# A product-key expert layer: who makes the low parts of the expert tables, and in what order

## The chip, the cores and the metric

The kernel runs on one core of a Trainium2 chip. Its time is the device time of one execution, in microseconds (us). TensorE multiplies matrices, VectorE, ScalarE and GpSimd work on elements, and SyncE starts most transfers. The engines run side by side and wait for each other by counters (semaphores).

## The reference, cut to what matters

Two layers of a network for 384 tokens (128 of context, 256 latent). Each layer ends with this channel mixer, and the change touches it alone:

```python
def peer_ffn(h, w_query, sub_keys, u_tab, v_tab):
    q = (h @ w_query).reshape(B, L, PEER_HEADS, 2, PEER_QDIM // 2)
    s = jnp.einsum('blhtd,htnd->blhtn', q, sub_keys)
    s1, i1 = lax.top_k(s[..., 0, :], PEER_TOPK)
    s2, i2 = lax.top_k(s[..., 1, :], PEER_TOPK)
    cand = s1[..., :, None] + s2[..., None, :]
    top, pos = lax.top_k(cand, PEER_TOPK)      # of the 16 x 16 sums
    idx = jnp.take_along_axis(cidx, pos, -1)   # expert = i1 * 128 + i2
    g = jax.nn.softmax(top, axis=-1)
    act = jax.nn.gelu(einsum('td,tkd->tk', h, u_tab[idx]))
    return einsum('tk,tkd->td', g * act, v_tab[idx])
```

There are 8 heads, 128 keys on each side, 16384 experts, 16 chosen for each head and token, and a width of 1024.

## The kernel before

The kernel gathers nothing. It computes the activation of all 16384 experts for all 384 tokens, multiplies by a gate that is zero for experts not chosen, and multiplies by the whole value table. The experts go in 128 blocks of 128.

**Split products.** Float32 precision is kept by splitting each operand into a high part (rounded) and a low part (the rest). ScalarE makes the high part of a table block (`high`), another engine the low part (`x - high`), and TensorE then does 24 matmuls for one block (`product`: 8 slices of the width, three products each, lines 976 to 978). Table buffers (`ur` loaded, `uh` high, `ul` low) and the PSUM result (`bank`) are doubled. Afterwards ScalarE applies the gelu and keeps the result in `A`, a ring of `RING` blocks (`gelu`, line 1070).

**The stages of one layer in `mix_experts`**, as TensorE goes through them:
1. 16 query blocks, each with its key scores (line 989). VectorE finds the top 16 as the scores come.
2. The first `FIRST` = 20 expert blocks (numbered from 0 here). Meanwhile VectorE *decodes* the chosen positions (`at_least`, `chosen`, `sum_ranks`, lines 1253 to 1286, "decoding"): large comparisons and sums in float16. Its last step posts `picked`.
3. Three transposes per token tile (line 1017), after which VectorE makes the operands of the gates.
4. The gates, in 48 chunks of 8 tokens. For each chunk VectorE makes *one-hots* in four instructions (`one_hots`, lines 1312 to 1316), TensorE multiplies them in 16 matmuls (`gates`, lines 998 and 999), and ScalarE copies the result out (line 1088) and stores it to memory after every eighth chunk. One block of the tables stands behind every 4 chunks: 12 groups, blocks 20 to 31.
5. A tail of 4 blocks, 32 to 35.
6. 128 *slots*: each multiplies the gated activations of a block by its values (line 1037, 18 matmuls), and in the first 92 slots one more table block (36 to 127) follows.

**Who makes the low parts.** GpSimd makes those of the query blocks and of blocks 0 to 36, in two halves (line 1173). VectorE makes those of blocks 37 to 127 whole, in the slots (`lo_part`, line 160).

**What sets the order.** Each engine runs its own list strictly as written; there is no scheduler. The waits that matter here: `product` of block n waits for its low part (`ulow`, or `ulow2` where VectorE makes it) and for the gelu of block n-2. One-hots are doubled, so `one_hots` of chunk c waits until TensorE has done chunk c-2 (`gated`). `gates` of chunk c waits for its one-hots (`hot`) and for the copy of chunk c-3. SyncE loads block n when the low part of block n-2 is made. ScalarE makes the high part of block n after product n-2.

Of the kernel before, what the change touches and what calls it, by code (L numbers as in the profile page):

```python
# [32 lines left out]
P = 128  # L33
D = 1024
KC = D // P
T = 384
# [770 lines left out]
FIRST, PER, TAIL = 20, 4, 4  # L807
RING = FIRST + NT * PER + TAIL
CT = 8
CHUNKS = P // CT  # L810
HALF = P // 2
SOON = 32
# [50 lines left out]
def mix_experts(nc, s, cx, d, layer, hi, lo, acc):  # L863
# [48 lines left out]
    with nc.Block() as block:  # L912
        @block.sync
        def _(sp):
# [18 lines left out]
            with sp.Fori(0, RING // 2) as i:  # L933
# [3 lines left out]
            sp.wait_ge(gst0, 16 * (NT + 1))  # L937
            value(0, 0)
            value(1, 1)
            sp.wait_ge(ulow, 2 * (J + RING) + 2)  # L940
            table(RING, 0)
            sp.wait_ge(gst1, 16 * (NT + 1))
            gate(0, 0)
            gate(1, 1)
            sp.wait_ge(ulow, 2 * (J + RING) + 4)
            table(RING + 1, 1)

            def slot(z):
                b = z.first % 2
                if z.has(RING + 2):  # L950
                    sp.wait_ge(ulow2, z.n + 1)
                    table(z.n + (RING + 2), b)
                if z.has(2):
                    sp.wait_ge(vlow, z.n + 3)
                    value(z.n + 2, b)
                    sp.wait_ge(applied, z.n + 1)
                    if z.first + 2 >= SOON:
                        sp.wait_ge(gst2, 16 * (NT + 1))
                    gate(z.n + 2, b)
# [4 lines left out]
        def _(pe):  # L964
# [39 lines left out]
            pe.sem_inc(gated, 2)  # L1004
# [20 lines left out]
            with pe.Fori(0, TAIL // 2) as i:  # L1025
                for b in range(2):
                    early(i * 2 + (J + RING - TAIL + b), b)

            def slot(z):
                b = z.first % 2  # L1030
                pe.wait_ge(vlow, z.n + 3)
                pe.wait_ge(wlow, z.n + 1)
                for t in range(NT):
                    w = slice(t * P, (t + 1) * P)
                    for lhs, rhs in ((wh, vh), (wh, vl), (wl, vh)):
                        for c in range(2):
                            mm = pe.matmul(acc[:, 2 * t + c, :], r32(lhs[:, b, w]), r32(rhs[:, b, c * 512:(c + 1) * 512]),  # L1037
                                           start=False, stop=False, skip_group_check=True)
                mm.then_inc(valued, 1)
                if z.has(RING):  # L1040
                    product(z.n + (J + RING), b, ulow2, z.n + 1, whole=True)
# [4 lines left out]
        def _(act):  # L1046
# [25 lines left out]
            def early(n, b, turn):  # L1072

                gelu(n + (J - 1), 1 - b, bass.ds(n - 1, 1))
                high(n + (J + 1), 1 - b, turn)

            def gates(t, u):
                c = t * CHUNKS + u
                if u == 0:
                    act.wait_ge(gst0, t * 16 + 16)  # L1080
                if u == CHUNKS // 2:
                    act.wait_ge(gst1, t * 16 + 16)
                    act.wait_ge(gst2, t * 16 + 16)
                act.wait_ge(gated, c + 3)
                at = u * CT % HALF
                out = stg[:, 2 * u // CHUNKS, :, at:at + CT].rearrange("p k t -> p t k")
                src = acc[:, 2 * (u % 3):2 * (u % 3) + 2, :].rearrange("p b (t k) -> p (b t) k", k=P)
                nc.scalar.activation(out, src, copy, scale=1.0 / GATE_SCALE).then_inc(evacd, 1)  # L1088
                if u == CHUNKS // 2 - 1:
                    act.wait_ge(evacd, c + 4)  # L1090
                    dst = gates_dram[bass.ds(t * 2, 1)].rearrange("a p k c -> p (a k) c")
                    act.dma_start(dst, stg[:, 0]).then_inc(gst0, 16)
                if u == CHUNKS - 1:
                    act.wait_ge(evacd, c + 4)
                    dst = gates_dram[bass.ds(t * 2 + 1, 1)].rearrange("a p k c -> p (a k) c")
                    act.dma_start(dst[:, 0:SOON], stg[:, 1, 0:SOON]).then_inc(gst1, 16)
                    act.dma_start(dst[:, SOON:NKEYS], stg[:, 1, SOON:NKEYS]).then_inc(gst2, 16)

            act.sem_inc(drained, 2)
            act.sem_inc(evacd, 3)  # L1100
            for g in (gst0, gst1, gst2):
                act.sem_inc(g, 16)
# [8 lines left out]
            high(J + 1, 1, J // 2)  # L1111
            with act.Fori(0, FIRST // 4) as i:
                for b in range(2):
                    early(i * 2 + (1 + b), 1 - b, i + (J // 2 + (2 + b) // 2))
            act.wait_ge(sub, 1)
            nc.scalar.activation(ex[:], ex[:], ACT.Exp).then_inc(expd, 1)
            nc.scalar.activation(warm[:], cx.eps[:], ACT.Gelu_apprx_tanh)
            done = FIRST // 4 * 2
            for n in range(done + 1, FIRST):
                early(n, n % 2, (n + 1 + J) // 2)  # L1120
# [3 lines left out]
            with act.Fori(0, NT) as t:  # L1124
                for a in range(PER):
                    early(t * PER + (FIRST + a), a % 2, t * (PER // 2) + (J + FIRST + a + 1) // 2)
                    for u in range(CHUNKS // PER):
                        gates(t, a * (CHUNKS // PER) + u)
# [14 lines left out]
            for n in range(RING - TAIL, RING):  # L1143
                if n == RING - 2:
                    value_high(start, 0)
                if n < RING - 1:
                    early(n, n % 2, (n + 1 + J) // 2)
            gelu(J + RING - 2, 0, bass.ds(RING - 2, 1))
            high(J + RING, 0, (J + RING) // 2, uhigh2)
# [17 lines left out]
        def _(pool):  # L1167
            pool.sem_inc(ulow, 4)
            with pool.Fori(0, (J + RING) // 2) as i:
# [6 lines left out]
        def _(dve):  # L1176
# [34 lines left out]
            find(J - 1, 1)  # L1211

# [58 lines left out]
            chosen(0)  # L1271
            st.done(v.tensor_tensor(pr[:], ge[:], table(1).unsqueeze(1).to_broadcast([P, T, TOPK]), ALU.mult))
            st.settle()
            sum_ranks(row[:])
            st.done(v.tensor_tensor(bd[:], posd[:], row[:].unsqueeze(2).to_broadcast([P, T, 2]), ALU.subtract))
            st.settle()
            at_least(bd, 2)
            chosen(1)
            dve.wait_ge(expd, 1)
# [7 lines left out]
                            den[:].unsqueeze(2).to_broadcast([P, TH, TOPK]), ALU.mult).then_inc(picked, 1)  # L1287
            dve.wait_ge(turned, 1)
# [14 lines left out]
            def one_hots(t, u):  # L1303
                c = t * CHUNKS + u
                b = u % 2
                toks = bass.ds(t * P + u * CT, CT)

                def each(x):
                    return x[:, toks, :].unsqueeze(2).to_broadcast(twos)

                dve.wait_ge(gated, c + 1)
# [27 lines left out]
            def table_low(z, ahead):  # L1339
                b = (z.first + ahead) % 2  # L1340
                dve.wait_ge(uhigh2, z.n + (ahead + 1))
                lo_part(nc, ul[:, b], ur[:, b], uh[:, b]).then_inc(ulow2, 1)

            dve.sem_inc(vlow, 2)
            start = Slot(0, 0)
            dve.wait_ge(evacd, NT * CHUNKS + 3)
            v.memset(acc[:], 0.0)
            value_low(start, 0)
            apply(start, 0)
            table_low(start, 0)  # L1350
            gated_low(start, 0)

            def slot(z):
# [4 lines left out]
                if z.has(RING + 1):  # L1358
                    table_low(z, 1)
# [776 lines left out]
```

## Time and profile before

| | us |
|---|---|
| median of 3 runs | 3905.05 (3904.53 to 3905.38) |
| the profiled execution | 3904.66 |
| its span, first to last instruction | 3902.9 |
| TensorE busy | 3271.5 (84%) |
| VectorE busy | 1951.1 (50%) |
| ScalarE busy | 1202.7 (31%) |
| GpSimd busy | 524.3 (13%) |
| mean granted clock of TensorE | 0.890 of full speed |

In the rows PE is TensorE, PEld its weight loads, DVE VectorE, ACT ScalarE, POOL GpSimd, SP SyncE. Matmul records overlap (a matmul is listed as 0.33 us where the next begins 0.17 us after it), so the pace is read from start to start. The clock has two levels, 0.5 (1.2 GHz) and 1.0 (2.4 GHz). The expert mixer of the first layer runs from 684 to about 1960 us, that of the second from about 2578.

### The profile page before, as it was taken

To read this page: it belongs to the slowest core of one execution; us is meant where nothing else is said; L and a number is where in the kernel's file an instruction comes from. 1 tells how busy PE (TensorE), PEld (TensorE's weight loads), DVE (VectorE), ACT (ScalarE), POOL (GpSimd) and SP (SyncE) were. 2 spreads that over 40 slices of the span, in tenths; PEclk is the share of its full clock that TensorE was granted. 3 is DMA by queue.
4 is the path that set the end of the run, shared out by engine and by line. 5 is a ranking of instruction groups with operands and counts; after the bars stand their busy time and mean duration, and the time that the engine had idled before them with its cause. 6 is when DMAs were issued, how large, how long until landed. Compare 5 with 4: busy or idle time off the path is not lost. (4 is left out here: it accounts for less than half of the span.)

```text
span 3902.9 us, 52370 instructions
## 1 busy us (share of the span) xinstructions
PE 3271.5 (84%) x17902; PEld 2844.6 (73%) x17902; DVE 1951.1 (50%) x3467; ACT 1202.7 (31%) x1789; POOL 524.3 (13%) x295
## 2 busy tenths in 40 slices
PE   8976384986799999999966456769769999999997
PEld 1275264976699999998855345769668999999986
DVE  0053435687644334444556787459773444334455
ACT  0011210445533333333322211134553333333333
POOL 0000000572200000000002664037321000000000
PEclk9987557997799999999985677879879999999999
DMA  8621001334544444444620000223345444444454
GB/s 298 236 97 62 3 3 65 109 97 162 192 149 152 154 153 150 149 149 143 177 80 3 14 5 3 87 82 107 140 167 181 148 147 152 153 153 151 150 156 120
DMA packets 297444, 478.06 MB, mean 122 GB/s; under 512 B 212480, under 2 KB 213248, under 8 KB 291216
## 3 DMA queue, kind: packets, MB, share of 16 engines
q1 hardware_dynamic: 294768, 426.68, 34.1%
q10 hardware_dynamic: 2592, 50.33, 3.1%
q8 instruction: 44, 0.72, 0.1%
q14 instruction: 40, 0.33, 0.0%
HBM read 424.19 MB, written 52.76 MB: 122 GB/s over the span
## 5 line engine op out<-in xcount | busy, mean ns | idle before, releaser
L976 PE MATMUL pe_s<-peer_hi,pe_uh 128*128 128x384 f32 x2304 | 796.4, 346 | 71.5 <-POOL pe_ul L1173 71.5
L160 DVE TENSOR_TENSOR val_vl<-val_vr,val_vh 128x1024 fp32r<-128x1024 f32 x256 | 313.8, 1226 | 1056.7 <-ACT val_vh L1134 1056.7
L977 PE MATMUL pe_s<-peer_lo,pe_uh 128*128 128x384 f32 x2304 | 785.5, 341 | 0.0
L978 PE MATMUL pe_s<-peer_hi,pe_ul 128*128 128x384 f32 x2304 | 784.8, 341 | 0.0
L976 PEld LDWEIGHTS pe_s<-peer_hi,pe_uh 128*128 128x128 f32 x2304 | 447.3, 194 | 85.2 <-issue 51.4
L1173 POOL TENSOR_TENSOR pe_ul<-pe_ur,pe_uh 128x512 fp32r<-128x512 f32 x208 | 334.2, 1629 | 1265.5 <-ACT pe_uh L1054 1265.3
L1070 ACT ACTIVATE pe_A<-pe_s 128x384 f32 (+1 forms) x256 | 126.1, 492 | 1200.0 <-PE pe_s L978 1200.0
L1037 PE MATMUL peer_acc<-val_vh,val_wl 128*128 128x512 f32 x1536 | 474.2, 390 | 0.0
L1037 PE MATMUL peer_acc<-val_vh,val_wh 128*128 128x512 f32 x1536 | 473.2, 389 | 0.0
L1037 PE MATMUL peer_acc<-val_vl,val_wh 128*128 128x512 f32 x1536 | 472.7, 389 | 0.0
L977 PEld LDWEIGHTS pe_s<-peer_lo,pe_uh 128*128 128x128 f32 x2304 | 446.6, 194 | 8.5
L978 PEld LDWEIGHTS pe_s<-peer_hi,pe_ul 128*128 128x128 f32 x2304 | 444.2, 193 | 0.0
L1037 PEld LDWEIGHTS peer_acc<-val_vl,val_wh 128*128 128x128 f32 x1536 | 288.4, 188 | 60.1
L1037 PEld LDWEIGHTS peer_acc<-val_vh,val_wl 128*128 128x128 f32 x1536 | 288.4, 188 | 59.7
L1134 ACT ACTIVATE val_vh<-val_vr 128x1024 fp32r<-128x1024 f32 x256 | 270.0, 1055 | 188.3 <-PE peer_acc L1037 176.2
L1037 PEld LDWEIGHTS peer_acc<-val_vh,val_wh 128*128 128x128 f32 x1536 | 285.7, 188 | 45.4
L998 PE MATMUL peer_acc<-gate_oh,gate_o 128*128 128x128 f16 x768 | 125.2, 257 | 126.4 <-DVE gate_ol L1316 126.4
L160 DVE TENSOR_TENSOR pe_ul<-pe_ur,pe_uh 128x1024 fp32r<-128x1024 f32 x184 | 225.4, 1225 | 0.0
L1088 ACT ACTIVATE gate_stg<-peer_acc 128x1024 f32<-128x1024 f32 x96 | 182.8, 1954 | 80.2 <-PE peer_acc L999 80.1
L1056 ACT ACTIVATE pe_uh<-pe_ur 128x1024 fp32r<-128x1024 f32 x184 | 193.7, 1053 | 0.4 <-DMA pe_ur<-in_peer_u 0.4
L998 PEld LDWEIGHTS peer_acc<-gate_oh,gate_o 128*128 128x128 f16 x768 | 88.3, 117 | 141.1 <-DVE gate_ol L1316 122.9
L204 PE MATMUL mod_acc<-mod_w,mod_sg 128*2 128x512 f32 x384 | 167.4, 596 | 14.9 <-DMA mod_w<-in_ada_w 14.9
(395 smaller groups left out, 4066.4 us busy)
## 6 DMA issues: line engine op xcount, KB each, us to landing
pe_ur<-in_peer_u SPq DMA_DIRECT2D x256, 512.0 KB, 3.8
val_vr<-in_peer_v SPq DMA_DIRECT2D x256, 512.0 KB, 4.4
mod_w<-in_ada_w SPq DMA_DIRECT2D x24, 2048.0 KB, 8.0
val_gr<-gates SPq DMA_DIRECT2D x256, 192.0 KB, 4.6
gates<-gate_stg ACTq DMA_DIRECT2D x6, 4096.0 KB, 11.5
gates<-gate_stg ACTq DMA_DIRECT2D x6, 3072.0 KB, 11.0
pe_ur<-in_w_query SPq DMA_DIRECT2D x32, 512.0 KB, 3.7
in_w<-in_w_in SPq DMA_DIRECT2D x18, 512.0 KB, 3.7
```

What stands on the lines that cost most here:

```text
L160: return nc.vector.tensor_tensor(r32(out), x, hi, ALU.subtract)
L204: mm = pe.matmul(acc[0:2, u, :], sg[:, k, :], w[:, u, k, :], start=k == 0, stop=k == KC - 1)
L976: pe.matmul(o, r32(uh[:, b, k]), r32(hi[:, k]), start=k == 0, stop=False)
L977: pe.matmul(o, r32(uh[:, b, k]), r32(lo[:, k]), start=False, stop=False)
L978: mm = pe.matmul(o, r32(ul[:, b, k]), r32(hi[:, k]), start=False, stop=k == KC - 1)
L998: pe.matmul(o, o1[:, u % 2, e], oh[:, u % 2, e], start=True, stop=False)
L1037: mm = pe.matmul(acc[:, 2 * t + c, :], r32(lhs[:, b, w]), r32(rhs[:, b, c * 512:(c + 1) * 512]), start=False, stop=False, skip_group_check ...
L1056: nc.scalar.activation(r32(uh[:, b]), ur[:, b], copy).then_inc(uhigh2, 1)
L1070: nc.scalar.activation(A[:, place, :].rearrange("p a t -> p (a t)"), bank[:, b, 0:T], ACT.Gelu_apprx_tanh).then_inc(drained, 1)
L1088: nc.scalar.activation(out, src, copy, scale=1.0 / GATE_SCALE).then_inc(evacd, 1)
L1134: nc.scalar.activation(r32(vh[:, b]), vr[:, b], copy).then_inc(vhigh, 1)
L1173: nc.gpsimd.tensor_tensor(r32(ul[:, b, h]), ur[:, b, h], uh[:, b, h], ALU.subtract).then_inc(ulow, 1)
```

## The change

It moves the low parts of blocks 6 to 36 from GpSimd to VectorE, made whole, and writes a new order. GpSimd keeps the query blocks and blocks 0 to 5. `FIRST` becomes 16, then 2 blocks (`HOLD`) stand between the transposes and the gates, and then one block behind every `GROUP` = 3 chunks: 16 groups, blocks 18 to 33. The tail is blocks 34 to 37, the ring has 38 places instead of 36, and the slots make blocks 38 to 127. The loops over token tiles are written out. The first value loads stand two blocks earlier among SyncE's table loads.

```diff
-FIRST, PER, TAIL = 20, 4, 4
-RING = FIRST + NT * PER + TAIL
-CHUNKS = P // CT
+CHUNKS = T // CT
+GROUP = 3
+LOW = 6
+FIRST, HOLD, TAIL = 16, 2, 4
+GATED = FIRST + HOLD
+LAST = GATED + CHUNKS // GROUP
+RING = LAST + TAIL
 ...
 TensorE
+            def late(n):
+                product(n + J, n % 2, ulow2, n - LOW + 1, whole=True)
-            with pe.Fori(0, FIRST // 2) as i:
+            with pe.Fori(0, LOW // 2) as i:
                 for b in range(2):
                     early(i * 2 + (J + b), b)
+            for n in range(LOW, FIRST):
+                late(n)
             pe.wait_ge(picked, 1)
 ...
-            with pe.Fori(0, NT) as t:
-                for u in range(CHUNKS):
-                    gates(t, u)
-                    if u % (CHUNKS // PER) == CHUNKS // PER - 1:
-                        a = u // (CHUNKS // PER)
-                        early(t * PER + (J + FIRST + a), a % 2)
+            for n in range(FIRST, GATED):
+                late(n)
+            for n in range(GATED, LAST):
+                for u in range(GROUP):
+                    gates((n - GATED) * GROUP + u)
+                late(n)
+            for n in range(LAST, RING):
+                late(n)
 ...
 VectorE
+            def table_low(n, b):
+                dve.wait_ge(uhigh2, n - LOW + 1)
+                lo_part(nc, ul[:, b], ur[:, b], uh[:, b]).then_inc(ulow2, 1)
+            between = iter(range(LOW, FIRST))
+            def fill():
+                n = next(between)
+                table_low(n, n % 2)
             at_least(posd, 0)
+            fill()
             chosen(0)
+            fill()
 ... (a fill in chosen too, before sum_ranks; 8 fills before picked)
+            for n in between:
+                table_low(n, n % 2)
+            table_low(FIRST, FIRST % 2)
 ...
-            with dve.Fori(0, NT) as t:
-                for u in range(CHUNKS):
-                    one_hots(t, u)
+            for c in range(CHUNKS):
+                one_hots(c)
+                if c % GROUP == 1:
+                    n = GATED - 1 + c // GROUP
+                    table_low(n, n % 2)
+            table_low(LAST - 1, (LAST - 1) % 2)
```

VectorE at the start of the decoding, before (`dec_ge`, `dec_pr` are the decoding's buffers, `ret_pick` its result):

```order
L1253 TENSOR_TENSOR dec_ge<-ret_posd,g_decode 128x6144
L1266 TENSOR_TENSOR dec_pr<-dec_ge,ret_dx 128x6144
L1259 TENSOR_TENSOR dec_pr<-dec_pr 128x384x8
L1259 TENSOR_TENSOR dec_pr<-dec_pr 128x384x4
L1259 TENSOR_TENSOR dec_pr<-dec_pr 128x384x2
L1262 TENSOR_TENSOR ret_pick<-dec_pr 128x384
L1272 TENSOR_TENSOR dec_pr<-dec_ge,g_decode 128x6144
```

and in the changed kernel (`pe_ul` is a low part of the table):

```order
L1256 TENSOR_TENSOR dec_ge<-ret_posd,g_decode 128x6144
L160 TENSOR_TENSOR pe_ul<-pe_ur,pe_uh 128x1024
L1269 TENSOR_TENSOR dec_pr<-dec_ge,ret_dx 128x6144
L160 TENSOR_TENSOR pe_ul<-pe_ur,pe_uh 128x1024
L1262 TENSOR_TENSOR dec_pr<-dec_pr 128x384x8
L1262 TENSOR_TENSOR dec_pr<-dec_pr 128x384x4
L1262 TENSOR_TENSOR dec_pr<-dec_pr 128x384x2
L1265 TENSOR_TENSOR ret_pick<-dec_pr 128x384
L160 TENSOR_TENSOR pe_ul<-pe_ur,pe_uh 128x1024
L1284 TENSOR_TENSOR dec_pr<-dec_ge,g_decode 128x6144
```

The first low part that VectorE makes (block 6) now stands behind the first large comparison, and nine more follow between the later steps.

VectorE in the gates, before, one chunk and the start of the next (the first row of a chunk is preceded by its wait; `REGISTER_ALU` and `ISA` set registers for the loop):

```order
L1312 TENSOR_TENSOR gate_eq<-g_iota,pe_i 128x1024
L1313 REGISTER_ALU
L1313 TENSOR_TENSOR gate_o<-g_iota,pe_i 128x1024
L1315 REGISTER_ALU
L1315 TENSOR_TENSOR gate_oh<-gate_eq,pe_gh 128x1024
L1316 REGISTER_ALU
L1316 TENSOR_TENSOR gate_ol<-gate_eq,pe_gl 128x1024
L1311 REGISTER_ALU
L1312 ISA
L1312 TENSOR_TENSOR gate_eq<-g_iota,pe_i 128x1024
```

and in the changed kernel, chunk 4 with the low part of block 18 behind it, and chunk 5:

```order
L1330 TENSOR_TENSOR gate_eq<-g_iota,pe_i 128x1024
L1331 TENSOR_TENSOR gate_o<-g_iota,pe_i 128x1024
L1333 TENSOR_TENSOR gate_oh<-gate_eq,pe_gh 128x1024
L1334 TENSOR_TENSOR gate_ol<-gate_eq,pe_gl 128x1024
L160 TENSOR_TENSOR pe_ul<-pe_ur,pe_uh 128x1024
L1330 TENSOR_TENSOR gate_eq<-g_iota,pe_i 128x1024
L1331 TENSOR_TENSOR gate_o<-g_iota,pe_i 128x1024
L1333 TENSOR_TENSOR gate_oh<-gate_eq,pe_gh 128x1024
L1334 TENSOR_TENSOR gate_ol<-gate_eq,pe_gl 128x1024
```

One low part now stands behind chunks 1, 4, 7 and so on up to 46, with three chunks between two of them.

ScalarE in the first groups, whose list shows the order in which TensorE delivers, before (`pe_A` is the gelu, `pe_uh` a high part, `gate_stg` a chunk copied out):

```order
L1070 ACTIVATE pe_A<-pe_s 128x384
L1074 REGISTER_ALU
L1054 ACTIVATE pe_uh<-pe_ur 128x512 x2
```

and in the changed kernel:

```order
L1079 ACTIVATE pe_A<-pe_s 128x384
L1065 ACTIVATE pe_uh<-pe_ur 128x1024
L1097 ACTIVATE gate_stg<-peer_acc 128x8x128 x3
L1079 ACTIVATE pe_A<-pe_s 128x384
L1065 ACTIVATE pe_uh<-pe_ur 128x1024
L1097 ACTIVATE gate_stg<-peer_acc 128x8x128 x3
```

Three chunks lie between two blocks of the tables, where four did.

## Rows read from the trace of the kernel before

**Rows 1.** Groups of instructions: line, engine, names, count, busy us, mean ns, idle before

```profile
L160 DVE TENSOR_TENSOR pe_ul<-pe_ur,pe_uh 128x1024 fp32r<-128x1024 f32 x184 | 225.4, 1225 | 0.0
...
L998 PE MATMUL peer_acc<-gate_oh,gate_o 128*128 128x128 f16 x768 | 125.2, 257 | 126.4 <-DVE gate_ol L1316 126.4
...
L1312 DVE TENSOR_TENSOR gate_eq<-g_iota,pe_i 128x1024 f16<-128x1024 f16 x96 | 66.6, 694 | 76.9 <-PE peer_acc L999 76.1 <-DVE pe_gl L1292 0.7
```

**Rows 2.** Windows, gates and decoding: length, busy PE, PEld, DVE, ACT, POOL, clock, DMA

```profile
862.50:1051.30 188.80, 127.98 (x1060) 120.87 (x1061) 144.92 (x193) 108.09 (x84) 39.84 (x24) 0.77 0.38 152
2757.10:2945.70 188.60, 127.58 (x1060) 120.47 (x1061) 145.13 (x193) 108.26 (x84) 40.23 (x24) 0.77 0.39 153
764.30:862.50 98.20, 88.09 (x491) 85.43 (x490) 84.53 (x282) 38.67 (x70) 75.95 (x40) 0.98 0.34 111
```

**Rows 3.** Timeline of TensorE in one gate group: start, duration, line, [idle <-releaser]

```profile
897.17 0.23 PE L998 MATMUL peer_acc<-gate_oh,gate_o 128*128 128x128 f16 x1
...
903.11 0.29 PE L998 MATMUL peer_acc<-gate_oh,gate_o 128*128 128x128 f16 x1 [3.97 <-DVE gate_ol L1316]
...
907.16 0.67 PE L976 MATMUL pe_s<-peer_hi,pe_uh 128*128 128x384 f32 x1
...
912.01 0.23 PE L998 MATMUL peer_acc<-gate_oh,gate_o 128*128 128x128 f16 x1
```

**Rows 4.** Timeline of VectorE in the same group

```profile
898.40 0.69 DVE L1312 TENSOR_TENSOR gate_eq<-g_iota,pe_i 128x1024 f16<-128x1024 f16 x1 [3.96 <-PE peer_acc L999]
899.01 1.76 DVE L1313 TENSOR_TENSOR gate_o<-g_iota,pe_i 128x1024 f16<-128x1024 f16 x1
...
902.97 0.68 DVE L1312 TENSOR_TENSOR gate_eq<-g_iota,pe_i 128x1024 f16<-128x1024 f16 x1
...
909.59 0.69 DVE L1316 TENSOR_TENSOR gate_ol<-gate_eq,pe_gl 128x1024 f16<-128x1024 f16 x1
```

**Rows 5.** Timeline of ScalarE: gelu of block 5, high part of 7, gelu of 7

```profile
789.74 0.49 ACT L1070 ACTIVATE pe_A<-pe_s 128x384 f32 x1 [2.64 <-PE pe_s L978]
...
790.13 1.15 ACT L1054 ACTIVATE pe_uh<-pe_ur 128x512 fp32r<-128x512 f32 x2
...
798.06 0.49 ACT L1070 ACTIVATE pe_A<-pe_s 128x384 f32 x1 [2.64 <-PE pe_s L978]
```

**Rows 6.** Timeline of VectorE: decoding, first and last steps, and the first one-hot

```profile
795.13 4.36 DVE L1253 TENSOR_TENSOR dec_ge<-ret_posd,g_decode 128x6144 f16<-128x6144 f16 x1
...
803.88 6.65 DVE L1259 TENSOR_TENSOR dec_pr<-dec_pr 128x3072 f16<-128x3072 f16 x3
...
846.29 1.59 DVE L1286 TENSOR_TENSOR ret_pick<-ret_ex,ret_den 128x384 f32<-128x384 f32 x1
...
862.57 0.69 DVE L1312 TENSOR_TENSOR gate_eq<-g_iota,pe_i 128x1024 f16<-128x1024 f16 x1 [0.35 <-DVE pe_gl L1292]
```

**Rows 7.** Timeline of GpSimd at the start of the decoding

```profile
790.83 2.54 POOL L1173 TENSOR_TENSOR pe_ul<-pe_ur,pe_uh 128x512 fp32r<-128x512 f32 x2 [1.63 <-ACT pe_uh L1054]
...
794.98 16.69 POOL L1173 TENSOR_TENSOR pe_ul<-pe_ur,pe_uh 128x512 fp32r<-128x512 f32 x6 [1.61 <-ACT pe_uh L1054]
```

**Rows 8.** Timeline of TensorE: products after waits, transposes, first slot

```profile
683.97 0.66 PE L976 MATMUL pe_s<-peer_hi,pe_uh 128*128 128x384 f32 x1 [25.13 <-POOL pe_ul L1173]
...
689.87 0.41 PE L976 MATMUL pe_s<-peer_hi,pe_uh 128*128 128x384 f32 x1
...
859.74 0.49 PE L1017 MATMUL peer_acc<-g_const,ret_pick 128*128 128x128 f32 x3
...
1067.05 0.69 PE L976 MATMUL pe_s<-peer_hi,pe_uh 128*128 128x384 f32 x1 [3.64 <-POOL pe_ul L1173]
...
1073.71 0.62 PE L1037 MATMUL peer_acc<-val_vh,val_wh 128*128 128x512 f32 x2
```

**Rows 9.** Timeline of ScalarE: the gelus of two slots that follow each other

```profile
1816.77 0.49 ACT L1070 ACTIVATE pe_A<-pe_s 128x384 f32<-128x384 f32 x1 [5.45 <-PE pe_s L978]
...
1825.03 0.49 ACT L1070 ACTIVATE pe_A<-pe_s 128x384 f32<-128x384 f32 x1 [5.45 <-PE pe_s L978]
```

More of the change, by code:

```diff
@@ L936, in _ @@
                     table(i * 2 + b, b)
[L937 to L946, printed above, removed]
+            for n in range(LOW + 2, RING + 2):
+                if n == RING - 2:
+                    sp.wait_ge(gst0, 16 * NT)
+                    value(0, 0)
+                    value(1, 1)
+                if n == RING:
+                    sp.wait_ge(gst1, 16 * NT)
+                    gate(0, 0)
+                    gate(1, 1)
+                sp.wait_ge(ulow2, n - 2 - LOW + 1)
+                table(n, n % 2)
             def slot(z):
@@ L1040, in slot @@
                 if z.has(RING):
-                    product(z.n + (J + RING), b, ulow2, z.n + 1, whole=True)
+                    product(z.n + (J + RING), b, ulow2, z.n + (RING - LOW + 1), whole=True)
             slots(pe, slot)
@@ new lines, in early, with gates @@
+            def early(n):
+                if n:
+                    gelu(n + J - 1, 1 - n % 2, bass.ds(n - 1, 1))
+                high(n + J + 1, 1 - n % 2, (n + J + 1) // 2, uhigh if n + 1 < LOW else uhigh2)
+            def gates(c):
+                part, at = c * CT // HALF, c * CT % HALF
+                half = part % 2
+                if at == 0 and part >= 2:
+                    act.wait_ge((gst0, gst1)[half], part // 2 * 16)
+                    if half:
+                        act.wait_ge(gst2, part // 2 * 16)
+                act.wait_ge(gated, c + 1)
+                out = stg[:, half, :, at:at + CT].rearrange("p k t -> p t k")
+                src = acc[:, 2 * (c % 3):2 * (c % 3) + 2, :].rearrange("p b (t k) -> p (b t) k", k=P)
+                nc.scalar.activation(out, src, copy, scale=1.0 / GATE_SCALE).then_inc(evacd, 1)
+                if at + CT == HALF:
+                    act.wait_ge(evacd, c + 1)
+                    dst = gates_dram[part]
+                    if half == 0:
+                        act.dma_start(dst, stg[:, 0]).then_inc(gst0, 16)
+                    else:
+                        act.dma_start(dst[:, 0:SOON], stg[:, 1, 0:SOON]).then_inc(gst1, 16)
+                        act.dma_start(dst[:, SOON:NKEYS], stg[:, 1, SOON:NKEYS]).then_inc(gst2, 16)
@@ L1110, in _ @@
             nc.scalar.activation(warm[:], cx.eps[:], ACT.Gelu_apprx_tanh)
[L1111 to L1120, printed above, removed]
+            for n in range(FIRST):
+                if n == FIRST // 2:
+                    act.wait_ge(sub, 1)
+                    nc.scalar.activation(ex[:], ex[:], ACT.Exp).then_inc(expd, 1)
+                    nc.scalar.activation(warm[:], cx.eps[:], ACT.Gelu_apprx_tanh)
+                early(n)
             act.wait_ge(turned, 1)
@@ L1123, in _ @@
                 nc.scalar.activation(dst[:], acc[:, 2 + k, 0:T].unsqueeze(2).to_broadcast([P, T, 2]), copy).then_inc(taken, 1)
[L1124 to L1128, printed above, removed]
+            for n in range(FIRST, GATED):
+                early(n)
+            for n in range(GATED, LAST):
+                early(n)
+                for u in range(GROUP):
+                    gates((n - GATED) * GROUP + u)
             def value_high(z, ahead):
@@ L1142, in _ @@
             start = Slot(0, 0)
-            for n in range(RING - TAIL, RING):
+            for n in range(LAST, RING):
                 if n == RING - 2:
                     value_high(start, 0)
[L1146 to L1149, printed above, removed]
+                early(n)
             gated_high(start, 0)
@@ L1168, in _ @@
             pool.sem_inc(ulow, 4)
-            with pool.Fori(0, (J + RING) // 2) as i:
+            with pool.Fori(0, (J + LOW) // 2) as i:
                 for b in range(2):
@@ L1337, in gated_low @@
                 lo_part(nc, wl[:, b], A[:, z.place(ahead), :].rearrange("p a t -> p (a t)"), wh[:, b]).then_inc(wlow, 1)
[L1339 to L1342, printed above, removed]
             dve.sem_inc(vlow, 2)
             start = Slot(0, 0)
-            dve.wait_ge(evacd, NT * CHUNKS + 3)
+            table_low(LAST, LAST % 2)
+            dve.wait_ge(evacd, CHUNKS)
             v.memset(acc[:], 0.0)
+            for n in range(LAST + 1, RING - 1):
+                table_low(n, n % 2)
             value_low(start, 0)
+            table_low(RING - 1, 1 - RING % 2)
             apply(start, 0)
-            table_low(start, 0)
             gated_low(start, 0)
+            table_low(RING, RING % 2)
             def slot(z):
@@ L1358, in slot @@
                 if z.has(RING + 1):
-                    table_low(z, 1)
+                    table_low(z.n + (RING + 1), 1 - z.first % 2)
             slots(dve, slot)
```

65 lines of the change are left out of this document (20 added, 45 removed).

## The prediction

> **What bounds the kernel now.** I read the busy times first: TensorE is busy 84% of the span, so the question is where it waits or runs slowly. The groups of instructions come next. TensorE waits 126.4 us for VectorE's one-hots in the gates, and VectorE waits 76.1 us there for TensorE's chunks [rows 1]. Each waits for the other, so neither is the bound alone: it is a chain through both. The windows show the place. The gates of a layer take about 188.7 us in both layers, with VectorE busy 145 us, TensorE 128 us and a mean clock of 0.77. The decoding ahead of them has TensorE busy 88 of 98.2 us at 0.98 [rows 2].
>
> The timelines show the chain of one group of four chunks and a block, some 15.5 us long (12 of them in the window of 188.8 us, with the start). At 897.17 TensorE starts two chunks whose one-hots were made while it did the product. VectorE may write the next one-hots when the first of the two is done, at 898.40. They take 4.6 us because two of the eight instructions meet GpSimd (1.76 us instead of 0.69). TensorE idles 3.97 us, does two more chunks, and the product starts at 907.16 [rows 3, 4]. So a product hides the one-hots of two chunks, and nothing hides the other two. In the slots ScalarE waits 5.45 us for TensorE in each round of 8.26 us: they are bound by TensorE, and a block moved out of them saves one product [rows 9].
>
> A product takes 4.16 us at the high clock (two gelus, two products apart: (798.06 - 789.74) / 2) [rows 5]. After an idle of 3.64 us it takes 6.66 us, as the clock is at its low level at first (1067.05 to 1073.71), and after 25 us of idling 18 of its 24 matmuls take 5.90 us, which makes 5.9 + 6 x 0.173 = 6.9 us [rows 8]. I use 6.66 behind a single long wait.
>
> **Decoding, part by part.** GpSimd loses the low parts of blocks 6 to 36 and VectorE gets them, at 1.23 us each [rows 1]. That is also what GpSimd needs for one half when undisturbed (2.54 us for two), and it takes 2.8 us for one in the decoding (16.69 us for six) [rows 7]. VectorE gains what the meetings cost it: 1.76 - 0.69 = 1.07 us for an instruction with two inputs [rows 4]. Decoding takes from 795.13 to 847.88 us, 52.75 us, with 19 such instructions [rows 6]. The trace shows none of the large ones without GpSimd. The bounds are 0 and 19 x 1.5 (GpSimd's longest hold is near its 1.27 us and the small ones seem to pay more) = 28 us; I take 19 x 1.07 = 20 us, so 32.4 us remain, plus 8 low parts of 1.23 = 9.8: `picked` at 837.3 instead of 847.9.
>
> A rule of the Trainium skill bears on this 20 us. "GPSIMD Engine Reference", section "Key points", says that GpSimd shares its SBUF interfaces with VectorE and collides with VectorE instructions that have two SBUF inputs. By it all 19 pay and the whole 20 us goes; the sum with nothing gained is a rival below.
>
> But the first low part now stands behind the first comparison, and TensorE needs it earlier. Block 5 ends at about 789.6, just ahead of its gelu [rows 5]; the comparison starts at 795.13 and takes 4.36 - 1.07 = 3.29 us, the low part 1.23: block 6 starts at 799.7, a new wait of 10.1 us. It takes 6.66 us, to 806.4. From there I go step by step: each low part follows its decoding step (3.3 us for a large one, 4.2 us for four of a sum) and the high part, which ScalarE ends 1.7 us after the product two before (gelu from 789.74, high part to 791.28, and 0.2 us ahead) [rows 5]; each product starts at the later of its low part and the product ahead. Blocks 7, 8 and 9 end at 810.6, 814.7 and 818.9. The low parts of 10 to 13 come at 819.5, 824.7, 829.3 and 834.8 and their products end 4.16 us later, 14 at 843.1, 15 at 847.3. Transposes take 1.1 us, to 848.4; until the first one-hot it takes 862.57 - 860.23 = 2.3 us, as before [rows 6, 8]. Two chunks of one-hots (8 x 0.602 = 4.8 us) and the low part of block 17 end at 856.8. Block 16 ended at 852.6, so TensorE idles 4.2 us, block 17 takes 6.66 us, and the first chunk starts at 863.5.
>
> **The gates.** This is the term that decides. An undisturbed one-hot instruction follows the next by (909.59 - 902.97) / 11 = 0.602 us [rows 4], 2.41 us for a chunk. VectorE's order is now one-hots of chunks 5, 6, 7, then the low part of block 19, while TensorE's is block 18, chunks 3, 4, 5, block 19. One-hots of chunk 5 wait for chunk 3, which stands behind block 18 on TensorE; block 19 waits for its low part, behind the one-hots of chunk 7. So in each group everything is in one chain:
> - product, 4.16 us at the high clock
> - from the first chunk's start until VectorE starts: 898.40 - 897.17 = 1.23 us [rows 3, 4]
> - three chunks of one-hots, 3 x 2.41 = 7.22 us
> - low part 1.23 us, and 0.1 us until TensorE starts.
>
> That is 13.9 us. While the product runs VectorE has nothing that it may do: the buffers of the two chunks it made ahead are not read yet. Before the product TensorE idles about 5 us, after a chunk alone between two gaps. The clock will be low when the product starts. Rows for its length are 4.85 us (907.16 to 912.01, a product behind a chunk, partly slow) [rows 3], 6.66 us after one wait of 3.64 us, 6.9 us after a long one [rows 8]. I take 6.2 us, nearer to the latter two. The group becomes 16.0 us. Removing the meetings with GpSimd is in it (no instruction at 1.76).
>
> The count: block 18 starts when the three chunks of one-hots and the low part are done, 863.5 + 1.23 + 8.55 = 873.3. 14 groups of 16.0 us later, at 1097.3, block 32 starts. The last group has only one chunk's one-hots ahead of block 33: 6.2 + 1.23 + 2.41 + 1.33 = 11.2, so 1108.5. Blocks 33 to 37 take 4.9 + 4 x 4.16 = 21.5 us, to 1130.0.
>
> The tail: the transfer of block 37 and the first gates queue behind the last gates' store; before, block 35 waited 3.64 us there [rows 8]. Bounds 0 and 3.6, with half of a slow product; I take 2 us. The slots start at 1132.0.
>
> Before they start at 1073.71 with 36 blocks done [rows 8]; now 38 are done, 2 x 4.16 = 8.3 us of later work. The first layer loses 1132.0 - 1073.7 - 8.3 = 50.0 us. The second repeats it (188.6 against 188.8 us in the gates [rows 2]): 100 us. Against the profiled execution of 3904.66 us that gives 4004.7, and against the median, 0.4 us higher, 4005.
>
> **Edits at nothing.** The low parts in the tail: VectorE is free and ScalarE's high part leads by a block. The loops written out: the 16 query blocks are written out already and run without a gap; uncovered it would show as idle time ahead of TensorE's instructions without a releaser. The earlier value loads are behind other work. High parts made whole instead of in halves (1.15 us for two [rows 5]) and the copies of the chunks lie behind the product and VectorE's chunks; ScalarE is busy 108 of 188.8 us before, with four copies in a group [rows 2], and gets three.
>
> **The rivals.**
> - *VectorE sets the pace* (the other side). If the one-hots of a group were made while the product runs, a group would cost only VectorE's work, 8.45 us. Block 33 would start at 873.3 + 15 x 8.45 = 1000, the slots at 1021.6, and the time would be 3905 - 2 x 60.4 = 3784. VectorE idle 3.96 us in each group even before [rows 4] speaks against it: it decides from a third one-hot buffer on, or a low part ahead of the one-hots, and the change has neither. 3%, with all partly faster cases 4%.
> - *The clock stays high* in the groups: 13.9 instead of 16.0, and blocks 6 and 17 at 4.16 us, 33 us less in a layer: 3939. The clock of 0.77 in the gates with idle times of 4 us speaks against it [rows 2]. 8%.
> - *The product is slow from end to end*, 24 x 0.328 = 7.9 us [rows 8], 1.7 us more in 14 groups of each layer: 4052. The six fast matmuls at the end of the product after 25 us of idling speak against it. 7%.
> - *The decoding gains nothing* from GpSimd's silence: `picked` 20 us later in each layer, 4045. 5%.
>
> [...]
>
> **How the numbers follow.** The forecast, 4005, holds 75%, with its own range 3970 to 4035 (6.2 us may be 5.4 to 6.9, 28 times, and the tail 0 to 3.6 twice). About 1% is left for no change, which a measurement tells within 0.2%. The range of 3945 to 4045 takes in the bounds of the product's length, and leaves out most of the fast-clock case, most of the slow one and the faster ones. Faster by over 0.2%: 0.04; within 0.2%: 0.01; slower: 0.95, from the forecast and the three rivals on its side.
>
> **What would show it.** In the gates, in TensorE's timeline: idle times of about 5 us ahead of each block's first matmul with VectorE's low part as releaser, 14 of them in a layer, and a group near 16 us. VectorE: an idle time of 6 to 8 us ahead of each third chunk's first one-hot, released by TensorE. No one-hot instruction above 0.7 us. In the decoding: one wait of 10 us ahead of block 6, `picked` near 837, comparisons of 3.3 us. GpSimd silent after block 5. The prediction is wrong if TensorE does not idle ahead of the blocks (the first rival), if products behind these waits take 4.2 or 7.9 us, or if gates start later than about 870 us.

## The result, and the profile after

| | before | after |
|---|---|---|
| median, us | 3904.79 (3902.41 to 3905.38, 4 runs) | 4031.13 (4030.49 to 4033.46, 4 runs) |
| ratio | | 1.0323 (95%: 1.0310 to 1.0336) |
| span of the profiled execution, us | 3902.9 | 4031.7 |

The change costs 126 us; 100 were forecast, by the mechanism that the trace now shows.

The groups of instructions after, in the columns of [rows 1]:

```profile
L982 PE MATMUL pe_s<-peer_hi,pe_uh 128*128 128x384 f32 x2304 | 817.1, 355 | 246.9 <-DVE pe_ul L160 196.4
...
L160 DVE TENSOR_TENSOR pe_ul<-pe_ur,pe_uh 128x1024 fp32r<-128x1024 f32 x244 | 297.0, 1218 | 38.6 <-ACT pe_uh L1065 38.1
...
L1330 DVE TENSOR_TENSOR gate_eq<-g_iota,pe_i 128x1024 f16<-128x1024 f16 x96 | 65.8, 686 | 247.6 <-PE peer_acc L1008 247.5
```

Each engine waits for the other, and for longer: VectorE 247.5 us for TensorE's chunks (76.1 before), TensorE 196.4 us for VectorE's low parts, a wait that the kernel before does not have (30 waits of 4.97 us in the gates make 149 us of it). TensorE's waits for one-hots fall from 126.4 to 54.3 us in return. Windows after: decoding and blocks 6 to 17, then 14 groups, then the last group and the tail up to the slots (the columns of [rows 2]).

```profile
799.72:865.43 65.71, 56.48 (x298) 54.26 (x298) 49.47 (x42) 20.51 (x28) 0.00 (x0) 0.93 0.33 97
875.12:1101.58 226.46, 133.08 (x1009) 126.44 (x1009) 118.25 (x182) 96.23 (x70) 0.00 (x0) 0.74 0.33 126
1101.58:1142.26 40.68, 34.29 (x192) 33.53 (x193) 14.83 (x15) 14.21 (x15) 0.00 (x0) 0.82 0.64 231
```

In the groups VectorE is busy 52% of the time, TensorE 59%, at a granted clock of 0.74. One engine works, then the other. One group in the timelines of TensorE and of VectorE, which answer to [rows 3, 4]:

```profile
907.11 0.66 PE L982 MATMUL pe_s<-peer_hi,pe_uh 128*128 128x384 f32 x1 [4.97 <-DVE pe_ul L160]
...
913.53 0.23 PE L1007 MATMUL peer_acc<-gate_oh,gate_o 128*128 128x128 f16 x1
...
917.18 0.23 PE L1007 MATMUL peer_acc<-gate_oh,gate_o 128*128 128x128 f16 x1 [1.70 <-DVE gate_ol L1334]
...
923.23 0.66 PE L982 MATMUL pe_s<-peer_hi,pe_uh 128*128 128x384 f32 x1 [4.97 <-DVE pe_ul L160]
```

```profile
905.75 1.22 DVE L160 TENSOR_TENSOR pe_ul<-pe_ur,pe_uh 128x1024 fp32r<-128x1024 f32 x1
914.63 0.69 DVE L1330 TENSOR_TENSOR gate_eq<-g_iota,pe_i 128x1024 f16<-128x1024 f16 x1 [7.67 <-PE peer_acc L1008]
...
921.87 1.22 DVE L160 TENSOR_TENSOR pe_ul<-pe_ur,pe_uh 128x1024 fp32r<-128x1024 f32 x1
```

Read them together: the low part ends at about 906.97 and VectorE then idles through the whole product (907.11 to 913.53) and the chunk behind it. It may write again at 914.63, makes three chunks of one-hots in 7.24 us and the low part, and TensorE starts the next product at 923.23, 16.12 us after the last. The 1.70 us ahead of the third chunk are inside VectorE's 7.24 us and cost nothing of their own.

### The profile page after: what moved, and what is told of

Read it like the earlier page. It is cut to its first block and busy times, and to the rows that moved or that the text cites. A ratio compares the mean times of both kernels' runs of the same rounds, so it can differ in the third digit from the quotient of the medians.

```text
span 4031.7 us, 51066 instructions
## 1 busy us (share of the span) xinstructions
PE 3300.1 (82%) x17902; PEld 2870.6 (71%) x17902; DVE 1929.7 (48%) x3527; ACT 1188.4 (29%) x1729; POOL 301.9 (7%) x175
## 5 line engine op out<-in xcount | busy, mean ns | idle before, releaser
L982 PE MATMUL pe_s<-peer_hi,pe_uh 128*128 128x384 f32 x2304 | 817.1, 355 | 246.9 <-DVE pe_ul L160 196.4
L983 PE MATMUL pe_s<-peer_lo,pe_uh 128*128 128x384 f32 x2304 | 807.2, 350 | 0.0
L984 PE MATMUL pe_s<-peer_hi,pe_ul 128*128 128x384 f32 x2304 | 804.9, 349 | 0.0
L982 PEld LDWEIGHTS pe_s<-peer_hi,pe_uh 128*128 128x128 f32 x2304 | 462.6, 201 | 264.9 <-issue 241.7
L984 PEld LDWEIGHTS pe_s<-peer_hi,pe_ul 128*128 128x128 f32 x2304 | 460.4, 200 | 0.0
L1046 PEld LDWEIGHTS peer_acc<-val_vl,val_wh 128*128 128x128 f32 x1536 | 288.3, 188 | 60.2
L160 DVE TENSOR_TENSOR pe_ul<-pe_ur,pe_uh 128x1024 fp32r<-128x1024 f32 x244 | 297.0, 1218 | 38.6 <-ACT pe_uh L1065 38.1
L1065 ACT ACTIVATE pe_uh<-pe_ur 128x1024 fp32r<-128x1024 f32 x244 | 256.6, 1052 | 35.2 <-DMA pe_ur<-in_peer_u 35.2
L1330 DVE TENSOR_TENSOR gate_eq<-g_iota,pe_i 128x1024 f16<-128x1024 f16 x96 | 65.8, 686 | 247.6 <-PE peer_acc L1008 247.5
L1172 POOL TENSOR_TENSOR pe_ul<-pe_ur,pe_uh 128x512 fp32r<-128x512 f32 x88 | 111.8, 1293 | 923.1 <-ACT pe_uh L1063 922.9
L1348 DVE TENSOR_TENSOR pe_A<-pe_A,val_gr 128x384 f32 (+1 forms) x256 | 141.5, 553 | 8.1 <-DMA val_gr<-gates 4.1
```

The costliest lines, as they stand in the source:

```text
L160: return nc.vector.tensor_tensor(r32(out), x, hi, ALU.subtract)
L982: pe.matmul(o, r32(uh[:, b, k]), r32(hi[:, k]), start=k == 0, stop=False)
L983: pe.matmul(o, r32(uh[:, b, k]), r32(lo[:, k]), start=False, stop=False)
L984: mm = pe.matmul(o, r32(ul[:, b, k]), r32(hi[:, k]), start=False, stop=k == KC - 1)
L1065: nc.scalar.activation(r32(uh[:, b]), ur[:, b], copy).then_inc(uhigh2, 1)
L1172: nc.gpsimd.tensor_tensor(r32(ul[:, b, h]), ur[:, b, h], uh[:, b, h], ALU.subtract).then_inc(ulow, 1)
```

## The experiments

"After" is the changed kernel. Ratios are to the kernel before, timed beside each run.

**A. The low part ahead of the one-hots.** The low part of a block is made one group of one-hots earlier; all else as after (`c` is the chunk whose one-hots VectorE has just made, `n` the block).

```
-                    n = GATED - 1 + c // GROUP
+                    n = GATED + c // GROUP
...
-            table_low(LAST - 1, (LAST - 1) % 2)      (behind the chunks)
+            table_low(GATED - 1, (GATED - 1) % 2)    (ahead of them)
```

> The changed kernel with each low part of the gates made one group earlier: VectorE makes that of block 17 before the first one-hots, and behind chunks 1, 4, 7 that of block 18, 19, 20. Theory (the chain product, chunk, three chunks of one-hots, low part is what costs): the product no longer waits for VectorE, TensorE starts block 19 behind chunk 5, and a group is product 4.16 + 1.23 + one chunk of one-hots 2.41 + 0.06 + chunk 0.98 = 8.9 us instead of 16.2, at the high clock; 15 groups and the start give some 116 us less in a layer: 3790 to 3810 us. Rival 1 (the 38 us of low parts that VectorE got are the loss, wherever they stand): 4000 or more. Rival 2 (ScalarE or the transfers bound a group of 3 chunks, with 10.5 us or more): 3850 or more.

3793.22 us, ratio 0.9710 (0.9690 to 0.9729). TensorE's timeline over a little more than one group, and VectorE's:

```profile
882.88 0.42 PE L982 MATMUL pe_s<-peer_hi,pe_uh 128*128 128x384 f32 x1
...
887.15 0.23 PE L1007 MATMUL peer_acc<-gate_oh,gate_o 128*128 128x128 f16 x1
...
890.81 0.23 PE L1007 MATMUL peer_acc<-gate_oh,gate_o 128*128 128x128 f16 x1 [1.70 <-DVE gate_ol L1335]
...
891.69 0.42 PE L982 MATMUL pe_s<-peer_hi,pe_uh 128*128 128x384 f32 x1
```

```profile
886.68 1.22 DVE L160 TENSOR_TENSOR pe_ul<-pe_ur,pe_uh 128x1024 fp32r<-128x1024 f32 x1
888.26 0.69 DVE L1331 TENSOR_TENSOR gate_eq<-g_iota,pe_i 128x1024 f16<-128x1024 f16 x1 [0.37 <-PE peer_acc L1008]
```

The same instructions, and only the place of the low parts in VectorE's list changed: the group falls from 16.18 us (the mean of after, (1101.58 - 875.12) / 14) to 8.81. The product no longer waits and takes 4.27 us. VectorE idles 0.37 us in place of 7.67: it is nearly the bound, at its 8.45 us of work. The chain through product, one-hots and low part was the whole loss, and more: 28 groups give 206 of the 238 us, and the first gated block starts 11.2 us earlier in a layer (863.90 for 875.12).

**B. The first eight low parts on GpSimd** (`LOW = 8` in place of 6).

> The changed kernel with GpSimd making the low parts of blocks 6 and 7 too (before the large comparisons begin). Theory: the wait of 10.3 us ahead of block 6 becomes one of about 1.9 us ahead of block 8 and nothing behind it takes the gain back, so the last block ahead of the transposes ends 8 to 9 us earlier in each layer: 4012 to 4016 us. Rival (VectorE's decoding sets the transposes, TensorE only waits elsewhere): unchanged within 4 us, 4029 us.

4010.19 us, ratio 1.0265 (1.0244 to 1.0285): 21 us less than after, and 2 below what I expected. The long wait ahead of block 6 (10.25 us in after) is a short one ahead of block 8:

```profile
799.39 0.41 PE L982 MATMUL pe_s<-peer_hi,pe_uh 128*128 128x384 f32 x1 [1.88 <-DVE pe_ul L160]
```

The gates start 9.6 us earlier in a layer (855.82 for 865.43) and their groups keep the 4.97 us.

**C. Both, A and B.**

> Both edits together: low parts one group ahead and GpSimd making those of blocks 6 and 7. Theory: the two gains lie in different stretches and add: 15 to 18 us below the run with the low parts ahead, 3775 to 3790 us. Rival (the second gain is swallowed by VectorE in the first gate groups): no more than 5 us below it.

3774.03 us (3772.25 to 3774.47, 4 runs), ratio 0.9661 (0.9645 to 0.9677), 19 us below A and 1 us below what I expected. The two gains add, so they lie in different stretches. It beats both kernels.

**D. After's order, with GpSimd making all low parts** (`LOW = RING`, VectorE makes none ahead of the slots), which separates the new order from the new engine.

> The changed kernel's order of blocks and chunks, with GpSimd making the low parts of all blocks ahead of the slots, in halves, as before. Theory (the loss comes from the low part standing in VectorE's list behind waiting one-hots, not from three chunks in a group): the product no longer waits for VectorE; a group is 4.16 + 1.23 + 2.41 + 2.15 (two meetings with GpSimd) + 0.06 + 0.98 = 11 us, with low clock in parts 12 to 12.5; the decoding is as long as before: 3870 to 3900 us. Rival (the new order with 16 groups of three chunks is the loss whoever makes the low parts): 4000 us or more.

3931.92 us, ratio 1.0065 (1.0044 to 1.0085): 32 us above the top of what I expected, but 99 below after. TensorE's and VectorE's timelines:

```profile
916.28 0.67 PE L982 MATMUL pe_s<-peer_hi,pe_uh 128*128 128x384 f32 x1
...
922.35 0.23 PE L1007 MATMUL peer_acc<-gate_oh,gate_o 128*128 128x128 f16 x1
...
928.14 0.29 PE L1007 MATMUL peer_acc<-gate_oh,gate_o 128*128 128x128 f16 x1 [3.84 <-DVE gate_ol L1328]
...
929.79 0.67 PE L982 MATMUL pe_s<-peer_hi,pe_uh 128*128 128x384 f32 x1
```

```profile
923.45 0.69 DVE L1324 TENSOR_TENSOR gate_eq<-g_iota,pe_i 128x1024 f16<-128x1024 f16 x1 [4.06 <-PE peer_acc L1008]
924.06 1.76 DVE L1325 TENSOR_TENSOR gate_o<-g_iota,pe_i 128x1024 f16<-128x1024 f16 x1
925.74 1.75 DVE L1327 TENSOR_TENSOR gate_oh<-gate_eq,pe_gh 128x1024 f16<-128x1024 f16 x1
```

The group takes 13.5 us, and it is another chain: the product (6.07), 1.10 us until VectorE starts, one chunk of one-hots (4.56, with two meetings with GpSimd at 1.76 us), the chunk that waited for them (0.13 and 1.65, slow), and the product again. Two of the three chunks of one-hots now lie beside the product. The chunk behind the 3.84 us of idle time and the product behind that chunk are slow, from the fourth gated block on: 0.8 and 1.8 us a group above their length in A, up to 28 x 2.6 = 73 us, more than the miss of 32. (Behind the same idle time the chunks ahead of the second and third gated blocks were fast, 0.88 and 0.93 us.) So neither the new order nor VectorE as the maker is the loss alone; it is the low part behind the one-hots, in that order. The new order with GpSimd as the maker is still 26 us slower than before, with GpSimd's meetings in it.

**E. A third buffer of one-hots.** To make room, the first comparison is written into the buffer in which it is multiplied, and two blocks go from behind the gates into the slots (`TAIL = 2`).

```
-        o1, eq, oh, ol = (x.sb(k, [P, 2, CT, P], F16) ...
+        o1, oh, ol = (x.sb(k, [P, 3, CT, P], F16) ...
...
-                if c >= 2:
-                    dve.wait_ge(gated, c - 1)
+                if c >= 3:
+                    dve.wait_ge(gated, c - 2)
```

> The changed kernel with three buffers for the one-hots instead of two, so that one-hots of chunk c wait for chunk c-3 only (the comparison is written where the high product goes, to save memory; the tail has 2 blocks instead of 4 and the ring 36). Theory: one chunk of one-hots moves beside the product; the chain is product, 1.23, two chunks of one-hots, low part: a group is 2.4 us shorter, 13.7 to 13.9 instead of 16.2, 70 us in both layers: 3955 to 3970 us. The rival of the prediction (from a third buffer on VectorE alone sets the pace, 8.5 us for a group): below 3850 us.

3950.94 us, ratio 1.0115 (1.0085 to 1.0144). Two products that follow each other:

```profile
900.07 0.66 PE L982 MATMUL pe_s<-peer_hi,pe_uh 128*128 128x384 f32 x1 [4.43 <-DVE pe_ul L160]
...
913.78 0.66 PE L982 MATMUL pe_s<-peer_hi,pe_uh 128*128 128x384 f32 x1 [4.44 <-DVE pe_ul L160]
```

A buffer takes one chunk of one-hots (2.41 us) out of the chain: the group falls by 2.5 us to 13.71, and 28 of them make 69 of the 80 us that the run gained. The other 11, and the 4 us that it lies below what I expected, were not followed; this run also has the shorter tail. The low part stays behind the one-hots and the product behind it.

**F. Narrow matmuls in the idle time**: 48 of 128 columns ahead of each gated block's product, values dropped.

> The changed kernel with 48 matmuls of 128 columns (their results are never read) ahead of the product in 15 of the 16 gate groups, where TensorE idles 5 us; 2.7 us at the high clock. Theory: the clock stays high, the products take 4.2 to 4.9 us instead of 5.6 to 7.1 (mean 6.3), the idle time ahead is otherwise the same: 1.5 to 2.1 us in 30 groups, 45 to 63 us: 3968 to 3986 us. Rival (the length of the product behind a wait is not a matter of what TensorE did before it): 4031 us or more.

4097.88 us, ratio 1.0491 (1.0447 to 1.0534). Groups of TensorE while one such set runs, then a window of it:

```profile
L1036 PE MATMUL peer_acc<-peer_hi 128*128 128x128 f32 x48 | 9.9, 400 | 0.0
```

```profile
912.50:922.30 9.80, 9.80 (x54) 9.80 (x51) 5.11 (x8) 2.77 (x2) 0.00 (x0) 0.54 0.89 374
```

They took twice the idle time and pushed the product back, so the run is 67 us slower than after and its time says nothing on the question. I had priced them at 2.7 us, 0.056 each. That is the pace of the gates' fp16 matmuls of 128 columns (in before 32 of them start from 897.17 to 898.92); these are fp32r and take 0.20. The question was put again, with other matmuls:

**G. Wide matmuls in the idle time.** In the product's own bank, values dropped; the product as it was behind them.

```
+                    pe.wait_ge(uhigh2, base)
+                    for k in range(3 * KC):
+                        pe.matmul(o, r32(uh[:, b, k % KC]), r32(hi[:, k % KC]), ...)
```

> The changed kernel, with 24 extra matmuls (384 columns, expert table's high part times query's high part, into the product's own bank, their values dropped) ahead of the product of each of the 15 gated blocks of a layer, issued behind the gates and ahead of the wait for the low part. At 0.173 us each they take 4.15 us and fit into the 4.97 us for which TensorE idles there, so they delay nothing. My theory: the product is slow (5.6 to 7.1 us in place of 4.2 to 4.4) because the engine stood idle before it, so with the idle time filled it takes 4.2 to 4.5 us, a group takes 14.0 to 14.4 us in place of 16.18, and 28 groups give back 50 to 60 us: 3970 to 3985. Rival: the product's length has another cause (the operands just written, the matrices' loads), then the time stays at 4028 to 4036; over 4036 the fillers come in the way, as in the run with narrow ones.

3962.11 us (3960.34 to 3963.42, 4 runs), ratio 1.0145 (1.0128 to 1.0162). TensorE's timeline of one group, and its window over 200 us of the gates (the same window of after has 118.45 us and a clock of 0.74):

```profile
912.51 3.74 PE L978 MATMUL pe_s<-peer_hi,pe_uh 128*128 128x384 f32 x20
...
917.58 0.44 PE L986 MATMUL pe_s<-peer_hi,pe_uh 128*128 128x384 f32 x1 [0.64 <-DVE pe_ul L160]
...
921.87 0.23 PE L1011 MATMUL peer_acc<-gate_oh,gate_o 128*128 128x128 f16 x1
```

```profile
880.00:1080.00 200.00, 165.42 (x1399) 156.02 (x1398) 122.47 (x188) 104.29 (x75) 0.00 (x0) 1.00 0.37 143
```

Work that is thrown away makes the kernel 69 us faster, 8 more than the top of what I expected. The product takes 4.29 us, the group 13.9 ((931.48 - 875.90) / 4 from four products on), and 28 x (16.18 - 13.9) = 64 us is nearly all of it. The order's own cost and the clock's are now apart.

**H. Real work in the idle time.** The 16 matmuls of a product that read only high parts go first, the wait for the low part stands ahead of the last 8. The edit takes in every product of which VectorE makes the low part, those of the slots too.

```
+                    for k in range(KC):
+                        pe.matmul(o, r32(uh[:, b, k]), r32(hi[:, k]), ...)
+                        pe.matmul(o, r32(uh[:, b, k]), r32(lo[:, k]), ...)
+                    pe.wait_ge(low, base)
+                    for k in range(KC):
+                        mm = pe.matmul(o, r32(ul[:, b, k]), r32(hi[:, k]), ...)
```

> The changed kernel, with the two thirds of every product that need no low part of the table (16 of its 24 matmuls) issued first and the wait for the low part put ahead of the last 8. In a gated block 16 x 0.173 = 2.77 us then go into the 4.97 us of idle time, and 8 are left behind it, 1.4 us at the high clock or 2.6 at the low one, in place of 5.6 to 7.1. My theory (the wait for the low part and the product behind it are in a row, and end what sets the group): the group falls from 16.18 us to 11.0 to 12.2, in 28 groups 111 to 145 us, and 3 to 8 us more at the waits of the decoding and of block 37: 3878 to 3917. Rival: VectorE's own chain sets the group, then less than 30 us are gained: over 4000.

3885.55 us (3882.56 to 3889.18, 4 runs), ratio 0.9951 (0.9935 to 0.9968): the same order of blocks and chunks as after, and 146 us less. One block in TensorE's timeline, and the same window as in G:

```profile
931.33 0.42 PE L978 MATMUL pe_s<-peer_hi,pe_uh 128*128 128x384 f32 x1
...
936.40 1.68 PE L982 MATMUL pe_s<-peer_hi,pe_ul 128*128 128x384 f32 x8 [2.02 <-DVE pe_ul L160]
```

```profile
880.00:1080.00 200.00, 147.53 (x1178) 135.74 (x1178) 131.12 (x192) 111.43 (x88) 0.00 (x0) 0.93 0.52 196
```

The idle time falls from 4.97 to 2.02 us and 1.5 us of product are left behind it (up to 2.4 in other groups), and the clock is at 0.93 on average. The group is 11.5 us ((936.40 - 878.84) / 5), which gives 28 x 4.7 = 131 of the 146 us. The gates also start 8.9 us earlier in a layer (856.53 for 865.43), as the waits of the decoding are shorter too. In the slots nothing is gained: a round there takes 8.26 us (1078.09 to 1086.35), as before [rows 9].

**I. C with H's product.**

> The kernel with both changes (low part ahead of the one-hots, the first eight low parts on GpSimd), with the same new order inside the product. There no product of a gated block waits for its low part (the group is 8.81 us, set by VectorE), so nothing is gained in it; what is left are the short waits of the decoding and the one ahead of the last block: 3765 to 3775, against 3774 without it. Rival: the 8.81 us hang on the product's end after all, then 10 us or more are gained.

3767.26 us (3766.09 to 3769.47, 4 runs), ratio 0.9644 (0.9628 to 0.9661). That is the fastest version run, 7 us below C: with no wait for low parts in the gates there is little left for it.

## Why the prediction was right, and where it fell short

- *The chain.* Right. A (nothing changed but the low part's place), G and H each shorten it at another member, and 28 times what the group lost gives 206 of 238 us in A, 64 of 69 in G and 131 of 146 in H.
- *A group of 13.9 us at the high clock.* Right to 0.05 us: G, where the clock is 1.00, has 13.9.
- *The product behind the wait, 6.2 us.* Slightly short. Products of after last 5.6 to 7.1 us, mean 6.5; the group was 16.18 for 16.0 (VectorE starts 1.10 us behind the first chunk's start, for 1.23). The 14 groups of a layer cost 2.5 us more than forecast.
- *Slow from end to end, 7.9 us.* Refuted; no product is. The product of 923.23 in after goes over to the high level with 7 of its 24 matmuls still to come. From there they start 0.17 us apart, in place of 0.32:

```profile
928.16 0.52 PE L982 MATMUL pe_s<-peer_hi,pe_uh 128*128 128x384 f32 x1
928.48 0.51 PE L983 MATMUL pe_s<-peer_lo,pe_uh 128*128 128x384 f32 x1
...
929.71 0.33 PE L983 MATMUL pe_s<-peer_lo,pe_uh 128*128 128x384 f32 x1
929.88 0.34 PE L984 MATMUL pe_s<-peer_hi,pe_ul 128*128 128x384 f32 x1
```

- *The clock stays high.* Refuted for after (0.74), and G shows what it would have been worth: 69 us, for which I had 66. That the two are so near is in part luck. My 66 had 10 us for blocks 6 and 17, which G leaves as they are; for the groups alone I had 28 x (6.2 - 4.16) = 57, and G gave 64.
- *VectorE sets the pace.* A shows it, at 8.81 for 8.45 us and 3793 for 3784 us. I had named two conditions, a third buffer or a low part ahead of the one-hots. The first is wrong: E frees one chunk of three. The second is right.
- *Decoding.* `picked` came at 838.3 for 837.3, the wait ahead of block 6 was 10.25 for 10.1, a comparison took 3.36 for 3.29, so the 20 us from GpSimd's silence were there, within 1 us. The small steps gave back as much as the large ones (the last one 1.59 before, 0.56 after). GpSimd was idle after block 5. But four steps of a sum take 4.9 us (804.01 to 808.92), for which I had 4.2, so the low parts of blocks 10 to 13 came 1.2 to 1.9 us late. TensorE waited 1.57, 1.12 and 1.61 us for three of them, where my steps had 0.4 to 1.3, and block 18 started at 875.12 for 873.3, 1.8 us. Block 6 took 5.54 us in place of 6.66, but that lead was lost in these waits.
- *The tail.* This is the step that failed in size. I had taken 21.5 us for blocks 33 to 37 and 2 us of wait for the transfer, 23.5; from block 33 to the first slot it takes 1142.26 - 1112.92 = 29.3 us. In the timelines of TensorE and of ScalarE in after:

```profile
1112.92 0.44 PE L982 MATMUL pe_s<-peer_hi,pe_uh 128*128 128x384 f32 x1 [0.16 <-DVE pe_ul L160]
...
1135.93 0.66 PE L982 MATMUL pe_s<-peer_hi,pe_uh 128*128 128x384 f32 x1 [4.54 <-DVE pe_ul L160]
```

```profile
1133.47 1.06 ACT L1065 ACTIVATE pe_uh<-pe_ur 128x1024 fp32r<-128x1024 f32 x1 [5.71 <-DMA pe_ur<-in_peer_u]
```

ScalarE waits 5.71 us for block 37's transfer, VectorE for ScalarE, TensorE for VectorE, and the product behind it is slow (6.33 us). The block that waits is the last one ahead of the slots. So was block 35 before, with its 3.64 us [rows 8], and I had bounded the new wait by that row. But it was the end of another wait. There ScalarE waited for the first value transfer, which its list had ahead of block 35's high part:

```profile
1063.56 1.06 ACT L1134 ACTIVATE val_vh<-val_vr 128x1024 fp32r<-128x1024 f32 x1 [6.90 <-DMA val_vr<-in_peer_v]
```

In after the value part had no wait (1124.75), and block 37's own transfer came last: issued at 1121.67, it took 11.8 us to land, where the median of these transfers is 3.6. So the row was no bound for it. The step cost 5.8 us: 4.9 from block 37's wait and slow product, 0.9 from blocks 33 to 36 (18.3 us for 17.4).

These make 1.8 + 2.5 + 0.1 (the last group) + 5.8 = 10.2 us in the first layer, 60.2 for 50.0 (its last value table's high part starts at 1972.00 before and at 2032.20 after). The second mixer lost 63.0 us; what its other 2.8 are was not followed. The layer between the two, which the change does not touch, took 4.3 us more in this execution (581.8 and 586.1 us, from that row to the root of the next norm). Over the eleven profiled executions, all with the same code there, it took 581.4 to 586.1, with B at 581.9 and C at 582.1, so that part varies from execution to execution and is not put down to the change. 60.2 + 4.3 + 63.0 and 1.3 us behind them make the 128.8 us between the spans. So the measured time lies in my own narrower range of 3970 to 4035, but only just, and 4.3 of its 26 us above the forecast are not the change's.

Two readings were wrong and did not enter the sum. The 4.6 us in the gates of before are one chunk of one-hots, four instructions of which two meet GpSimd, and not eight (898.40 to 902.97). And before, GpSimd made the low parts of blocks 0 to 35, not 36: it ran 208 instructions, two for each of 16 + 36 blocks in two layers. The change moves 30 blocks in a layer, as VectorE's count shows (184 in [rows 1], 244 in after).

What stays open is why the length of the slow product varies from 5.6 to 7.1 us from one group to the next, behind the same idle time of 4.97 us. The lengths repeat every four groups, in both layers (7.1, 5.7, 6.4, 6.9, then 7.1 again), so it is no noise. And that block 37's transfer queues behind the store was not tried. The trace shows only that the DMA engines are full while it waits (share 1.01, 386 GB/s from 1115.00 to 1133.50), with the last store issued at 1115.51.

## What to carry to other kernels

When two engines feed each other, write the cycle down as a chain and ask for each piece of work whether the other engine could be doing something meanwhile; a piece moved onto an engine that already waits lengthens the chain if it stands behind work that waits for the other engine, and may leave it ahead of that work (7.4 us of a group here, for one place in the order). It then counts only in the work of its own engine, which was nearly the bound in A. Here a buffer more helped by one chunk of three, and the place in the order by the whole wait. Before waiting for the last operand, issue the part of the work that does not need it: in H it filled idle time and raised the clock from 0.74 to 0.93 (the two gains were not measured apart).

## What I had not expected of the hardware

- Thrown-away matmuls in the idle time pay for themselves (G), but not any: the 48 narrow ones of F, 128 columns wide in fp32r, take 9.7 us (912.59 to 922.31), 0.20 us each, more than the 0.173 us of 384 columns at the high clock. The granted clock was 0.54 while TensorE was busy with them without a gap, and the product behind them started slowly. How much of the 0.20 us is the low clock and how much the width was not tried.
- In D a wait of 3.84 us stands ahead of 16 short fp16 matmuls. From the fourth gated block on they are slow (1.65 us for 0.88), and the product behind them is nearly as slow as if it had waited itself (6.07 us).
